# A streaming encoder step on one core: consumers of key scores and attention heads placed further behind their producers

## The reference

```
h = rmsnorm(x, g1);  z = h @ w_in            # one projection, cut into GLA and FoX parts
o_gla = gla_recurrence(gq, gk, gv, log_a)    # 4 heads, chunked linear attention
o_fox = softmax(q k^T * scale + c_t - c_s, causal) @ v        # 8 heads of 64
x = x + concat(o_gla_normed, o_fox) @ w_out
# PEER: 8 heads, each picks 16 of 128*128 experts
q = rmsnorm(x, g2) @ w_peer_q                # per head two halves of 128
s1, i1 = top_k(q1 . subkeys1, 16);  s2, i2 = top_k(q2 . subkeys2, 16)
top, ti = top_k(s1[:, None] + s2[None, :], 16);  idx = e1 * 128 + e2
g = softmax(top)
y = x + sum_k g_k * gelu(u_tab[idx_k] . h) * v_tab[idx_k]     # 128 experts a row
```

## Time and profile before

| | |
|---|---|
| median of three runs | 3522.37 us |
| the profiled execution, its own time | 3523.86 us |
| its span (first to last instruction) | 3522.1 us |
| PE busy | 2743.5 us (78%) |
| DVE busy | 2567.4 us (73%) |
| ACT busy | 1500.5 us (43%) |
| POOL busy | 1270.4 us (36%) |
| moved by DMA | 1287.09 MB, mean 365 GB/s |
| gathers, of it | 1112.08 MB |

### The profile page before, as it was taken

One profiled execution on the slowest core, in us unless ns is written; L12 is line 12 of the kernel. 1 busy time (PEld: TensorE's weight loads), 2 busy tenths in 40 slices (PEclk: granted clock), 3 DMA queues, 4 the chain that ended last, 5 costly groups with the idle time before them and its releaser, 6 DMA issues. The chain is left out here.

```text
span 3522.1 us, 33822 instructions
## 1 busy us (share of the span) xinstructions
PE 2743.5 (78%) x9149; PEld 1604.5 (46%) x9149; DVE 2567.4 (73%) x5555; ACT 1500.5 (43%) x3900; POOL 1270.4 (36%) x1070
## 2 busy tenths in 40 slices
PE   7858878777887886777878887767887788777767
PEld 5736545333654453334644454334553445333322
DVE  1286655898668877887668777887667767888775
ACT  2343354444324744443236644444235553444433
POOL 0023312333343443333434443323333434444343
PEclk9979978988898998987988898888998989888899
DMA  8498957999998999998999999878998999999998
GB/s 307 171 346 344 392 210 295 373 345 351 370 421 342 398 415 393 346 335 340 422 411 341 411 410 415 334 297 358 422 421 317 405 357 418 421 421 406 362 410 365
DMA packets 189479, 1287.09 MB, mean 365 GB/s; under 512 B 24184, under 2 KB 25992, under 8 KB 37608
## 3 DMA queue, kind: packets, MB, share of 16 engines
q0 software_dynamic: 153360, 1112.08, 79.2%
q1 hardware_dynamic: 31160, 166.84, 11.9%
q10 hardware_dynamic: 4768, 6.00, 0.5%
HBM read 1262.74 MB, written 22.10 MB: 365 GB/s over the span
## 5 line engine op out<-in xcount | busy, mean ns | idle before, releaser
L1279 PE MATMUL ps_acc<-uv_ring,coef_diag 128*128 128x512 f32 x2648 | 1512.5, 713 | 644.6 <-ACT coef_diag L970 630.3
L697 POOL DMA_INDIRECT uv_ring<-in_peer_uv,expert_index x1056 | 1260.2, 1193 | 2046.7 <-PE ps_acc L1279 1807.1
L1631 DVE CUSTOM_DVE_ANT_0 uv_ring<-uv_ring,h_rows 128x1024 f32<-128x1024 f32 x1056 | 1281.2, 1220 | 418.9 <-DMA uv_ring<-in_peer_uv,expert_index 412.8
L1279 PEld LDWEIGHTS ps_acc<-uv_ring,coef_diag 128*128 128x128 f32 x2648 | 561.0, 224 | 1359.7 <-ACT coef_diag L970 810.2
L965 ACT ACTIVATE gelu_u_dot_h<-u_dot_h 128x2 f32<-128x2 f32 x528 | 107.2, 203 | 1278.4 <-DVE u_dot_h L1631 1277.0
L1639 DVE SCALAR_TENSOR_TENSOR v_sums<-uv_ring,coefficients,v_sums 128x1024 f32<-128x1024 f32 x394 | 505.2, 1282 | 41.0 <-ACT coefficients L972 41.0
L1061 PE MATMUL ps_scores<-weight_chunk,rows_T 128*128 128x256 f32 x1728 | 418.3, 399 | 11.0 <-DMA weight_chunk<-in_w_in_chunks 11.0
L1061 PEld LDWEIGHTS ps_scores<-weight_chunk,rows_T 128*128 128x128 f32 x1728 | 347.6, 202 | 104.1 <-issue 41.6
L1250 PE MATMUL ps_scores<-weight_chunk,rows_T 128*128 128x256 f32 x1152 | 267.7, 387 | 2.2 <-DMA weight_chunk<-scratch_keys_w 1.4
L970 ACT ACTIVATE coef_diag<-coef_diag,gelu_u_dot_h 128x128 f32<-128x128 f32 x662 | 251.1, 398 | 17.5
L1250 PEld LDWEIGHTS ps_scores<-weight_chunk,rows_T 128*128 128x128 f32 x1152 | 224.9, 195 | 68.5 <-issue 38.4
(11 more groups left out here) (193 smaller groups left out, 2213.1 us busy)
## 6 DMA issues: line engine op xcount, KB each, us to landing
weight_chunk<-in_w_in_chunks SPq DMA_DIRECT2D x60, 1024.0 KB, 9.0
weight_chunk<-scratch_keys_w SPq DMA_DIRECT2D x40, 1024.0 KB, 9.0
weight_chunk<-in_w_out_chunks SPq DMA_DIRECT2D x20, 1024.0 KB, 9.0
uv_ring<-in_peer_uv,expert_index POOLq DMA_INDIRECT x1056, 11.2
uv_ring<-in_w_peer_q_T SPq DMA_DIRECT2D x8, 1024.0 KB, 9.2
rows_T<-in_x_T SPq DMA_DIRECT2D x9, 512.0 KB, 5.9
x_mid<-in_x_rows SPq DMA_DIRECT2D x9, 512.0 KB, 10.0
scratch_xm<-x_mid SPq DMA_DIRECT2D x9, 512.0 KB, 12.8
```

The costliest lines, as they stand in the source:

```text
L697: pool.indirect_dma_start(out=ring[:, s % RING, :], out_offset=None, in_=dram["uv"], in_offset=bass.IndirectOffsetOnAxis(ap=idx[:, t % IDX ...
L1279: mm = pe.matmul(acc[:, c, :], diag[:, r, :], ring[:, r, D + c * 512:D + (c + 1) * 512], start=first, stop=False, skip_group_check=True)
L1631: dve.tensor_tensor_reduce(out=ring[:, s % RING, 0:D], in0=ring[:, s % RING, 0:D], in1=h2[:], scale=1.0, scalar=0.0, op0=ALU.mult, op1=ALU ...
```

## The change

Distances between the engines grow; what is computed stays.

- Routing, counted from the unit's key scores: copy at step 10 (2 before), VectorE's chain from 14 (4), floats of the indices 21 (8), exponentials 25 (13), numbers 29 (17), reciprocal 29 and out of the chain (15, in the chain), weights 32 (17). A unit still starts every 16 steps, so two or three units are now under way at once. A route stage has 33 - 16 = 17 steps more than 16 for each unit, where it had 4; the due slot of a unit is set by its step 33 (19 before).
- Attention of tiles 0 to 3: two steps instead of one between the engines of a head (`lag`). Scores stand at 4+3h, maximum 6+3h, exponentials 8+3h, transposes 10+3h, copy 12+3h, product 14+3h. From tile 4 on the distance stays one, and 32 or 33 steps stand where 33 stood (42 for tiles 0 to 3).
- The planner's weights for attention are spread over the new count of steps. `PROLOGUE` is 131 steps (108 before); it ends in the same place of the work, with two units routed.

The core of the diff:

```diff
-ATT_STEPS = 33
-CHAIN_AT, KEYS_AT, EXP_AT = 4, 8, 13
+SCORES_AT, CHAIN_AT, KEYS_AT, EXP_AT = 10, 14, 21, 25
+NUMBER_AT, INVERSE_AT, WEIGH_AT = 29, 29, 32
+UNIT_ENDS = WEIGH_AT + 1
 def route_steps(ts):
-    return UNIT * PH * len(ts) + 4
+    return UNIT * (PH * len(ts) - 1) + UNIT_ENDS
+def lag(t):
+    return 2 if t < 4 else 1
+def value_at(t):
+    return 7 * lag(t) + 3 * (FH - 1) + (quads(t) - 1) // 2
+def att_steps(t):
+    return value_at(t) + 3 * lag(t) + 1
...
-                due.append((base + UNIT * m + UNIT + 3, SLOTS * t + slots_of(t) // PH * j))
+                due.append((base + UNIT * m + UNIT_ENDS, SLOTS * t + slots_of(t) // PH * j))
...
-                h, r = divmod(n - 4, 3)
+                h, r = divmod(n - 4 * lag(t), 3)
-                    hh, rr = divmod(n - 6 - q // 2, 3)
+                    hh, rr = divmod(n - 6 * lag(t) - q // 2, 3)
-                m, r = divmod(step - 2, UNIT)
+                m, r = divmod(step - SCORES_AT, UNIT)
-                m, r = divmod(step - EXP_AT - 4, UNIT)
+                m, r = divmod(step - NUMBER_AT, UNIT)
+                if r == 0 and 0 <= m < PH * len(ts):
+                    j, i = divmod(m, len(ts))
+                    act.wait_ge(picked, base + m + 1)
+                    number(ts[i], j)
+                m, r = divmod(step - WEIGH_AT, UNIT)
...
-                h, r = divmod(n - 2, 3)
+                h, r = divmod(n - 2 * lag(t), 3)
-                    hh, rr = divmod(n - 5 - q // 2, 3)
+                    hh, rr = divmod(n - 5 * lag(t) - q // 2, 3)
-                    hh, rr = divmod(n - 7 - q // 2, 3)
+                    hh, rr = divmod(n - 7 * lag(t) - q // 2, 3)
...
-            dve.wait_ge(tex, n + 1)
-            wait(dve, weighed, n)
-            dve.reciprocal(pinv[:], psum_[:]).then_inc(pin_r, 1)
+        def inverse(n):
+            dve.wait_ge(tex, n + 1)
+            wait(dve, weighed, n)
+            dve.reciprocal(pinv[:], psum_[:]).then_inc(pin_r, 1)
+                m, r = divmod(step - CHAIN_AT, UNIT)
+                if r == 0 and 0 <= m < PH * n:
+                    j, i = divmod(m, n)
+                    chain_of = router(ts[i], j)
+                m, r = divmod(step - INVERSE_AT, UNIT)
+                if r == 0 and 0 <= m < PH * n:
+                    inverse(base + m)
```

More of the change, by code:

```diff
@@ L1153, in attend @@
             done = tiles_before(bi + 1)
-            for n in range(ATT_STEPS):
+            for n in range(att_steps(t)):
                 if n == 0:
@@ L1189, in attend @@
                         value(t, hh, q)
-                if n == ATT_STEPS - 2:
+                if n == value_at(t) + 2 * lag(t):
                     pe.wait_ge(o_n, t + 1)
@@ L1483, in attend @@
             i = PLACE[t][1]
-            for n in range(ATT_STEPS):
-                h, r = divmod(n - 3, 3)
+            for n in range(att_steps(t)):
+                h, r = divmod(n - 3 * lag(t), 3)
                 if r == 0 and 0 <= h < FH:
```

23 lines of the change are left out of this document (11 added, 12 removed).

## The result

The changed kernel takes 3380.91 us (median of four runs, 3371.72 to 3388.98) against 3517.61 us for the kernel before in the same session (four runs): a ratio of 0.9607, interval 0.9572 to 0.9643, 3.9% faster. 3425 us were predicted.

The account below looks back on a forecast made before the run. Route stages were taken as bound by VectorE's waits, mostly for ScalarE's copy, other stretches by bytes or a chain through the engines. Gains 58 + 12 + 22 + 5 = 97 us from 3523.86 gave 3427, predicted as 3425 us, range 3380 to 3475.

Parts of the forecast that it names:

- What bounds it: Whole kernel: VectorE's waits limit route stages, bytes the 421 GB/s stretches, a chain through all engines attention of tiles 1 and 2.
- The shift of the front by the tail: Route stages: 13 more tail steps shift about three slots from the projection stage; costed at nothing.
- The residual wait of the copy, 18 us: Three route stages: part of VectorE's 85.1 us of waits that stays, as ScalarE's copy queues behind gelu; 18 us.
- Gather waits, 9 us: Three route stages: faster dots sometimes find their gather not landed; 3 us a stage lost, 9 us.
- Last route stage, 12 us: 3019 to 3475 us: gain from the copy's wait of 22.6 us, limited by bytes to 17; 12 us taken.
- First routing, 5 us: 191 to 270 us: VectorE's 8.1 us wait for the copy shrinks; gain 5 us (0 to 8).
- Attention of tiles 1 and 2, 22 us: 470 to 565 us: TensorE's 20.5 us of waits go and the clock may help; gain 22 us (5 to 40).
- Attention of tile 3, 0 us: Attention of tile 3: bound by bytes, so no gain; 0 us.
- (a): Route stages: gathers take the wait's place, routing gives nothing; 3495 us, chance 0.08.
- (b): Route stages: the copy waits in ScalarE's own list, half of the 85 us stays; 3471 us, chance 0.12.
- (c): Last route stage: numbers come too late for the gathers, GpSimd waits, kernel slower; 3585 us, chance 0.04.
- (d): Whole kernel: more comes back, VectorE without a gap, attention 40 us; gain 160 us, 3362 us, chance 0.16.

Follow-up runs that it names:

- e4: Changed kernel with VectorE's chain and all that follows three steps earlier, chain one step behind the copy: 3409.2 us, ratio 0.9688 to the kernel before.
- e5: Kernel before with the new attention and new plan (longer tail, new dues), routing at its old distances: 3462.53 us, ratio 0.985.
- e2: Kernel before with only the new attention distances; old routing distances, tail and dues: 3502.53 us, ratio 0.9957.
- e10: Kernel before with new attention and new dues (none past the stage's end), old routing distances and tail: 3502.44 us, ratio 0.9958.
- e1: Changed kernel with every tile's attention back at one step between engines, new routing kept: 3408.0 us, ratio 0.969 to the kernel before.
- e11: Changed kernel with 16 more steps of tail in every route stage: 3400.9 us, ratio 0.9683 to the kernel before.
- e7: Changed kernel with VectorE's adds in every other group outside projection and attention stages given to TensorE: 3319.2 us, ratio 0.9449 to the kernel before.
- e15: e11 with VectorE's maximum of seven tile 8 heads two slots behind its scores instead of one: 3401.23 us, ratio 0.9669 to the kernel before.

## Why the prediction was right and wrong

**What bounds it: right.** VectorE's waits for the copy were what the route stages lost, and the third kind of stretch, attention at a low clock, was a chain. The stretches at 421 GB/s kept their length (69.9, 71.9 and 69.5 us before, 70.7, 72.6 and 69.9 now for the same slots). The working gives no number for what stood behind that wait, ScalarE's own 71.1 us of waiting for TensorE's scores; by e4 it was most of it.

**The shift of the front by the tail: wrong, and the step that mattered.** "I cost the shift at nothing", with at most 3 slots x 3 stages x 1 us if the cover failed. e5 against e2 shows 38 us, the largest miss of the sum. I had looked at what the tail holds (no chain work) and not at what it moves: where every later step falls among the slots. It comes as 16 to 17 us in the route stages (820.1 and 818.9 us against 836.4), 11 to 16 in the attention of tiles 7 and 8, and 10 in the last stage through the dues. Cut at the same 80 slots each, the route stages hold less of the next stage's work on VectorE once the tail is in them: busy 723.0 us in the three in e2, 711.8 in e5; 723.2 before, 709.7 in the changed kernel. Little of it comes back behind them: slots 184 to 341 take 467.9 us in e2 and 470.1 in e5.

**The residual wait of the copy, 18 us: wrong.** 0.4 us was measured. With it the route stages' idle time on VectorE fell by 74.7 us (110.2 to 35.5, cut at slots) where 58 stood; the other 13.5 us of their 88 are the work that left with the tail. I had allowed VectorE one dot, 1.3 us, between gelu and chain. The timeline of the changed kernel shows what else stands there (start, length, engine, line, operation):

```profile
616.44 0.20 ACT L984 ACTIVATE gelu_u_dot_h<-u_dot_h 128x2 f32<-128x2 f32 x1 [5.31 <-DVE u_dot_h L1660]
...
617.38 0.18 ACT L941 ACTIVATE neg_top<-expert_top 128x1 f32<-128x1 f32 x1
...
617.59 1.28 ACT L944 ACT_TABLE_LOAD   x1
...
618.62 1.28 DVE L1668 SCALAR_TENSOR_TENSOR v_sums<-uv_ring,coefficients,v_sums 128x1024 f32<-128x1024 f32 x1
618.88 0.31 ACT L944 ACTIVATE top_exp<-expert_top,neg_top 128x16 f32<-128x16 f32 x1
...
619.19 0.36 ACT L931 ACTIVATE mixing_or_attention<-ps_scores 128x256 f32<-128x256 f32 x1
...
619.82 0.74 DVE L1595 TENSOR_TENSOR mixing_or_attention<-expert_pair,iota 128x512 f32<-128x512 uint32 x1
...
620.59 0.69 DVE L1600 TENSOR_TENSOR mixing_or_attention<-mixing_or_attention,key_top_index_f 128x512 f32<-128x512 f32 x1
...
621.31 0.69 DVE L1605 TENSOR_REDUCE expert_index_f<-mixing_or_attention 128x16 f32<-128x512 f32 x1
621.92 1.22 DVE L1660 CUSTOM_DVE_ANT_0 uv_ring<-uv_ring,h_rows 128x1024 f32<-128x1024 f32 x1
...
623.13 0.47 DVE L1554 MAX8 key_top<-mixing_or_attention 128x8 f32<-128x128 f32 x2
```

The copy is done at 619.55. VectorE still has the last third of the unit before to do, comparison, product and sum (L1595, L1600, L1605), 2.1 us that no longer wait for anything, and the chain begins at 623.13. In the 48 units the median from the copy's end to the chain's start is 2.0 us, where it was 0.03. With units overlapping, the tail of one covers the head of the next; I had counted only what the slots put between them. e4 agrees: with the chain three steps nearer, where that work no longer lies in between, 18.7 us of wait come back; it moves the chain and takes the work away at once, so what each is worth is not told apart. The written order of VectorE's list shows these instructions before any run.

**Gather waits, 9 us: the right kind, half the size.** The dot waits 17.8 us in the three stages, where it was 4.5, and is the largest wait left in each; the rate is 379 to 392 GB/s, where 386 stood in the working.

**Last route stage, 12 us: near in size by luck, wrong in cause.** 9.8 us, but they come with the dues (e10 447.4) and not with the distances (e5 446.6, changed kernel 446.1).

**First routing, 5 us: the same.** 8.9 us by the profile; e5 with the old distances has them too (68.7 us, and a wait for the copy of 3.0 us instead of 8.1).

**Attention of tiles 1 and 2, 22 us: right.** 26.0 us in the profile, 27 by e1, 15 alone (e2); 68.6 us and a clock of 0.90 where about 73 and over 0.75 were named. ScalarE did not stop it: it is busy 46.4 of 69 us with 15 table loads of 1283 ns. By the Trainium skill ("ScalarE: Activation LUTs", What ACT_TABLE_LOAD costs), with its drain of 1.38 us for each of them it would have needed 46 + 21 = 67 us, an estimate. The trace disagrees: in the rows above ScalarE's instruction ahead of the load ends at 617.56, the load takes 617.59 to 618.87, and the exponential starts at 618.88. 260 of the 362 loads in that trace stand like this, with less than 0.1 us idle on either side, so there is no room for 1.38 us.

**Attention of tile 3, 0 us: wrong.** It takes 9 us more (66.1 to 75.3), while the rate there falls from 413 to 376 GB/s and the clock from 0.97 to 0.86. With the new attention and the old plan it takes 68.9 us (e2), with the old attention and the new plan 71.1 (e1), with both 75.4 (e5), and with the longer tail of e11 67.0. The cause is not shown.

**The rivals.** (a) fell: the rate reached 379 to 392 GB/s in the route stages and 416 in e7. That is above the 358 GB/s that the Trainium skill ("DMA: Bandwidth & Descriptors", Specifications) gives as one core's limit of HBM; the same page (Measured) gives that figure for two cores that stream at once, and this program runs on one. (b) fell: the chain's wait for the copy is 0.4 us. Its sum says that half of the 85 us stays, which is 42, and puts 35 without saying what takes the rest. (c) fell: GpSimd's wait for numbers isn't among its waits of 872 to 1040 any more. (d) was the nearest to what happened, 3362 us against 3381, though with another cause for part of it: it named no gain by the plan.

Put together by ratios, in this order: attention 15 (e2), plan 38 (e5 to e2), routing distances 85 (changed kernel to e5), of it 75 in the route stages. Taken in another order the parts differ: attention on top of the rest is 27 (e1).

## What to carry to other kernels

In lists that several engines run through in a fixed order, place a consumer a few slots behind its producer: on an engine that is full, each wait of a few us is lost for all that stands behind it. Count the distance along the whole chain, from the engine that starts it (here TensorE) to the full one (VectorE): the engine between may wait, or the full one may stand right behind it, but not both. Where units overlap, ask what of the unit before stands ahead of the wait, not only what the spacing inserts. And when a distance changes a length or a due, price the plan by itself (old distances, new plan): a shift of one slot for everything that follows can be worth as much as the edit. When the waits are gone, weigh the load again: 121 adds moved from VectorE to TensorE were worth 62 us (what they would give in the kernel before was not run).

## What was not expected of the hardware

The granted clock rose where TensorE had more to do. e7's route stages have it busy 204 of 230 to 237 us at a clock of 0.97 to 0.99; the changed kernel's 186 of 246 to 252 at 0.89 to 0.91; the attention of tiles 1 and 2 went from 0.69 to 0.90 while its busy share went from 76% to 80%; e11 and e15, which make TensorE wait in tile 8, stand at 0.82 and 0.79 there, where the changed kernel has 0.90. A v matmul takes 616 ns in e7's third stage and 706 in that of the changed kernel. In these stretches a wait of TensorE came together with slower matmuls, and its going with faster ones. The tie is not strict: e5 takes the same time as the changed kernel for tile 8 (120.3 us) at 0.87. The DMA rate held 410 to 416 GB/s through route stages of 230 us and more with gathers of 8 KB rows beside the weights.
